# First attention of a two-block transformer: value scratch by token tiles, odd heads' halves swapped when staged, first key load earlier, weight fetches and single operations behind steps

## What is computed

```python
h = rmsnorm(x, g_mix[i])
z = h @ w_in[i]
zb, zc, zx, zq, zk, zv = jnp.split(z, ...)            # 6 x 512 columns
y_c = zb * causal_dwconv3(zc * zx, conv_w[i], conv_b[i])
q = rmsnorm(zq.reshape(b, t, 8, 64), q_norm_g[i])
k = rmsnorm(zk.reshape(b, t, 8, 64), k_norm_g[i])
v = zv.reshape(b, t, 8, 64)
y_a = dilated_attention(q, k, v).reshape(b, t, 512)
y = jnp.concatenate([rmsnorm(y_c, g_out_conv[i]), rmsnorm(y_a, g_out_attn[i])], axis=-1)
x = x + y @ w_out[i]
# then a gated FFN with a causal convolution, a gated per-token embedding,
# and a second block (sparse attention and retention, output product, FFN)
```

## Time and profile before

| | before |
|---|---|
| median of 3 runs | 2587.49 us (2584.89 to 2587.68) |
| profiled execution, its own time | 2583.64 us |
| its span | 2582.0 us |
| busy: PE, DVE, ACT, POOL | 2516.0, 1361.7, 1055.3, 1265.2 us |
| moved by DMA, mean rate | 246.28 MB, 95 GB/s |
| share of PE in the chain that ended last | 87% |

### The profile page before, as it was taken

The page is one execution under the profiler, slowest core; times in us unless marked ns, Lnnn a source line. Parts: engine busy times, 40 slices in busy tenths (PEclk is TensorE's granted clock), DMA queues, the critical chain, the costliest instruction groups (busy, mean ns, idle before and its releaser), DMA issues.

```text
span 2582.0 us, 34606 instructions
## 1 busy us (share of the span) xinstructions
PE 2516.0 (97%) x12210; PEld 2088.5 (81%) x12210; DVE 1361.7 (53%) x2479; ACT 1055.3 (41%) x1951; POOL 1265.2 (49%) x940
## 2 busy tenths in 40 slices
PE   8989999999999999999999999889999999999999
PEld 6877878888888888888877777689888888888887
DVE  5327766188766762225267888777247333333222
ACT  6336653253333332224256666586234333322120
POOL 2122323457766665534525554454356666656441
PEclk9999999999999999999999999999999999999999
DMA  4253432312222244210323212320412222226311
GB/s 157 75 170 117 116 82 83 146 58 106 90 82 88 77 160 175 82 65 27 107 74 94 66 62 70 108 69 21 155 74 74 82 85 79 82 105 222 114 45 70
DMA packets 107402, 246.28 MB, mean 95 GB/s; under 512 B 18880, under 2 KB 40672, under 8 KB 106976
## 3 DMA queue, kind: packets, MB, share of 16 engines
q1 hardware_dynamic: 107232, 244.08, 27.9%
HBM read 184.27 MB, written 55.05 MB: 93 GB/s over the span
## 4 chain that ended last, share of the span: by engine, by line
PE 87%; DVE 4%; ACT 2%; issue 2%; DMA 2%; POOL 2%; SPq 1%; ACTq 0%; DVEq 0%; POOLq 0%
PE PS L965 10%; PE PS L964 10%; PE PS L963 10%; PE PS L701 8%; PE PS L703 8%; PE PS L702 8%; PE PS L981 6%; PE PS L982 6%; PE PS L983 6%; PE PS L1233 2%; PE PS L1213 1%; PE PS L806 1%; PE PS L933 1%; PE PS L935 1%; PE PS L934 1%
## 5 line engine op out<-in xcount | busy, mean ns | idle before, releaser
L701 PE MATMUL PS<-Hh,Wl 128*128 128x512 f32 x1072 | 434.3, 405 | 12.0 <-DVE Hl L1364 9.4
L703 PE MATMUL PS<-Hh,Wh 128*128 128x512 f32 x1072 | 420.7, 392 | 0.0
L702 PE MATMUL PS<-Hl,Wh 128*128 128x512 f32 x1072 | 420.3, 392 | 0.0
L3220 POOL TENSOR_TENSOR Wl<-Wr,Wh 128x512 fp32r<-128x512 f32 (+1 forms) x158 | 209.4, 1346 | 336.0 <-ACT Wh L2320 335.7
L3323 POOL TENSOR_TENSOR RG<-RW,RG 128x512 fp32r<-128x512 f32 x176 | 246.9, 1408 | 130.2 <-ACT RG L2631 130.0
L1807 DVE TENSOR_TENSOR XA<-PS,XA 128x512 f32<-128x512 f32 x192 | 132.4, 691 | 332.5 <-PE PS L983 332.5
L981 PE MATMUL PS<-Hh,RG 128*128 128x512 f32 x704 | 274.1, 389 | 1.6 <-POOL Hl L3419 1.2
L983 PE MATMUL PS<-Hh,RG 128*128 128x512 f32 x704 | 273.9, 389 | 0.0
L982 PE MATMUL PS<-Hl,RG 128*128 128x512 f32 x704 | 273.9, 389 | 0.0
L3323 POOL TENSOR_TENSOR RG<-SW,RG 128x512 fp32r<-128x512 f32 x120 | 165.3, 1377 | 171.5 <-ACT RG L2631 147.0
L965 PE MATMUL PS<-Hh,RG 128*128 128x512 f32 x640 | 249.0, 389 | 0.0
(11 more groups left out here) (365 smaller groups left out, 5145.6 us busy)
## 6 DMA issues: line engine op xcount, KB each, us to landing
RW<-in_wg SPq DMA_DIRECT2D x44, 512.0 KB, 3.7
RW<-in_wu SPq DMA_DIRECT2D x44, 512.0 KB, 4.6
R<-in_wd SPq DMA_DIRECT2D x88, 256.0 KB, 3.0
hgscr<-GB SPq DMA_DIRECT2D x44, 512.0 KB, 2.6
G<-hgscr SPq DMA_DIRECT2D x40, 512.0 KB, 6.8
Wr<-in_wi SPq DMA_DIRECT2D x27, 512.0 KB, 3.4
Wr<-in_wo SPq DMA_DIRECT2D x16, 512.0 KB, 3.3
spill<-X SPq DMA_DIRECT2D x16, 512.0 KB, 2.6
```

What stands on the lines that cost most here:

```text
L701: pe.matmul(ps(b), k.Wl[:, s, wc], xh[:, kx, sl], start=kk == 0, stop=False)
L702: pe.matmul(ps(b), k.Wh[:, s, wc], xl[:, kx, sl], start=False, stop=False)
L703: i = pe.matmul(ps(b), k.Wh[:, s, wc], xh[:, kx, sl], start=False, stop=kk == nk - 1)
L3220: i = pool.tensor_tensor(k.Wl[:, s, c], k.Wr[:, s, c], k.Wh[:, s, c].bitcast(F32), ALU.subtract)
```

## The change

It touches only the first attention and the conv around it. Values: the scratch is laid out by token tile, [tile][token][8 heads x 128], so a store is one row of 896 elements per partition, and every head's load is one DMA of 8 pieces of 128 elements per partition; the swapped order of odd heads is made when VS is written (DVE's one instruction becomes two). SP: `key_load(1)` stands ahead of the values' stores instead of at the first step of `tables1`; the fetch of a unit goes from ahead of c into the tile of half 1 (after its first tick); the store of YC goes into the next j. ACT: `use()` goes from ahead of c into the tile of half 0 (after its first tick); the exponential goes ahead of `next_head`; `key_high` is two halves, at i = 3 and i = 4; the squares go later. DVE: the first tap goes into the tile ("b", 0) and the taps one place on, the second of them into ("b", 1); `conv_b` goes into the tile that follows its own. j = 3 keeps its order. POOL's additions follow the squares.

```diff
@@ vector
     for i in range(8):
         dve.wait_ge(*at("v", i))
         dve.wait_ge(*at("vt_hi", i))
-        dve.scalar_tensor_tensor(out=k.VS[i][:, :, 1, :], in0=ps(i).rearrange("p (h n) -> p h n", h=8),
-                                 scalar=k.sml[:, 112 + i:113 + i], in1=k.VS[i][:, :, 0, :].bitcast(F32), op0=ALU.mult,
-                                 op1=ALU.subtract).then_inc(*up(("free", i), "vt", i))
+        for e in range(2):
+            m = dve.scalar_tensor_tensor(out=k.VS[i][:, e::2, 1 - e, :],
+                                         in0=ps(i).rearrange("p (h n) -> p h n", h=8)[:, e::2, :],
+                                         scalar=k.sml[:, 112 + i:113 + i], in1=k.VS[i][:, e::2, e, :].bitcast(F32),
+                                         op0=ALU.mult, op1=ALU.subtract)
+        m.then_inc(*up(("free", i), "vt", i))
...
         dve.tensor_tensor(zs, ps(b), zs, ALU.mult).then_inc(*up(("free", b), "zx", j, half))
-        if half == 0:
-            return
+
+    def conv_first(j):
         y = k.YC[:, j % 2, :]
...
-                taps = {2: lambda j=j: conv_tap(j, 1), 6: lambda j=j: conv_tap(j, 0)} if (c, half) == ("b", 0) else {}
-                walk(8, 2, taps, tick)
+                later = {}
+                if (c, half) == ("c", 0) and j:
+                    later = {2: lambda j=j, b=b: conv_b(j - 1, 1, b)}
+                if (c, half) == ("b", 0):
+                    if j < 3:
+                        later = {2: lambda j=j: conv_first(j), 6: lambda j=j: conv_tap(j, 1)}
+                    else:
+                        later = {2: lambda j=j: conv_tap(j, 1), 6: lambda j=j: conv_tap(j, 0)}
+                if (c, half) == ("b", 1) and j < 3:
+                    later = {2: lambda j=j: conv_tap(j, 0), 4: lambda j=j, b=b: conv_b(j, 0, b)}
+                walk(8, 2, later, tick)
...
@@ scalar
-        act.activation(k.KSa[h % 2][:, :], k.KSr[:, :], ACT.Copy).then_inc(*up("q_hi", "k1_hi", h))
+        key_part(h, 0)
+        key_part(h, 1).then_inc(*up("q_hi", "k1_hi", h))
+
+    def key_part(h, z):
+        if z == 0:
+            act.wait_ge(*at("k1_in", h, 1))
+        return act.activation(k.KSa[h % 2][:, half_of(z)], k.KSr[:, half_of(z)], ACT.Copy)
...
+        if i == 3 and h < 7:
+            key_part(h + 1, 0)
         if i == 4 and h < 7:
-            key_high(h + 1)
+            key_part(h + 1, 1).then_inc(*up("q_hi", "k1_hi", h + 1))
...
-            if s < n:
-                next_head(s)
             if 1 <= s <= n:
                 e = s - 1
...
+            if s < n:
+                next_head(s)
...
         for c in "cxb":
-            use()
             for half in range(2):
-                walk(8, 2, {}, tick)
+                later = {}
+                if half == 0:
+                    later[2] = use
+                if (c, half) == ("c", 0) and j:
+                    later[6] = lambda j=j: conv_square(j - 1, 1)
+                walk(8, 2, later, tick)
                 b = bank.next()
+                if (c, half) == ("b", 1) and j < 3:
+                    conv_square(j, 0)
...
@@ sync
-        to, src = k.V2[h % 2][:, :, :].bitcast(F32), k.vs[h].rearrange("p (c n) -> p c n", c=8)
-        if h % 2 == 0:
-            sp.dma_start(to, src).then_inc(*up(("d_s", h), "v2_in", h))
-            return
-        for z in range(2):
-            sp.dma_start(to[:, :, 64 - 64 * z:128 - 64 * z], src[:, :, 64 * z:64 * z + 64]).then_inc(
-                *up(("d_s", h), "v2_in" if z else "v2_hi_in", h))
+        src = k.vs.rearrange("c p n -> p c n")[:, :, 128 * h:128 * h + 128]
+        sp.dma_start(k.V2[h % 2][:, :, :].bitcast(F32), src).then_inc(*up(("d_s", h), "v2_in", h))
...
-            if i == 0 and h < 7:
+            if i == 0 and 0 < h < 7:
                 key_load(h + 1)
...
+    key_load(1)
     for i in range(8):
...
-        sp.dma_start(k.vs.rearrange("h p n -> p h n")[:, 1:8, 128 * i:128 * i + 128],
-                     v[:, 128:1024].rearrange("p (h n) -> p h n", h=7)).then_inc(*up(("d_y", i), "v_kept", i))
+        sp.dma_start(k.vs[i][:, 128:1024], v[:, 128:1024]).then_inc(*up(("d_y", i), "v_kept", i))
...
         for c in "cxb":
-            use()
             for half in range(2):
-                walk(8, 2, {}, bg.tick)
+                walk(8, 2, {2: use} if half else {}, bg.tick)
```

More of the change, by code:

```diff
@@ L1568, in vector @@
                     conv_x(j, half, b)
+                    if (j, half) == (3, 1):
+                        conv_first(3)
                 if c == "b":
-                    conv_b(j, half, b)
                     if j == 3:
+                        conv_b(j, half, b)
                         add("conv", 3, half, k.sq_no["conv", half, 3])
@@ L2472, in key_high @@
     def key_high(h):
-        act.wait_ge(*at("k1_in", h, 1))
-        act.activation(k.KSa[h % 2][:, :], k.KSr[:, :], ACT.Copy).then_inc(*up("q_hi", "k1_hi", h))
+        key_part(h, 0)
[4 more added lines that the diff above has]
+        return act.activation(k.KSa[h % 2][:, half_of(z)], k.KSr[:, half_of(z)], ACT.Copy)
     def query_high(h, half):
@@ L2497, in scalar @@
         act.wait_ge(*at("rstd", "mix", i // 4))
-        act.activation(k.VS[i][:, :, 0, :], ps(i).rearrange("p (h n) -> p h n", h=8), ACT.Copy,
+        act.activation(k.VS[i][:, :, :, :].rearrange("p (c e) z n -> p c (e z) n", e=2)[:, :, 0:4:3, :],
+                       ps(i).rearrange("p (c e n) -> p c e n", c=4, e=2), ACT.Copy,
                        scale=k.sml[:, 112 + i:113 + i]).then_inc(*up("hn_a", "vt_hi", i))
@@ L2587, in scalar, with conv_square @@
     bg.add(attention1_norm())
+    def conv_square(j, half):
+        staged = [("v2_in", 0, 7), ("v_kept", 7)] if (j, half) == (1, 0) else []
+        square("conv", j, half, k.YC[:, j % 2, half_of(half)], staged + [("yb", j, half)])
     def y_high(half):
@@ L2599, in scalar @@
         for c in "cxb":
-            use()
             for half in range(2):
-                walk(8, 2, {}, tick)
+                later = {}
[4 more added lines that the diff above has]
+                walk(8, 2, later, tick)
                 b = bank.next()
+                if (c, half) == ("b", 1) and j < 3:
+                    conv_square(j, 0)
                 if c == "b":
-                    staged = [("v2_in", 0, 7), ("v_kept", 7)] if (j, half) == (1, 0) else []
-                    square("conv", j, half, k.YC[:, j % 2, half_of(half)], staged + [("yb", j, half)])
                     if j == 3:
+                        conv_square(3, half)
                         y_high(half)
@@ L3304, in gpsimd @@
                 walk(8, 2, {}, bg.tick)
-                if c == "b" and 0 < j < 3:
-                    add("conv", j, half)
-                    pool.wait_ge(*at("acc", "conv", half, j))
+                if (c, half) == ("b", 1) and 0 < j < 3:
+                    add("conv", j, 0)
+                    pool.wait_ge(*at("acc", "conv", 0, j))
+                if (c, half) == ("c", 0) and 0 < j - 1 < 3:
+                    add("conv", j - 1, 1)
+                    pool.wait_ge(*at("acc", "conv", 1, j - 1))
                 if (c, j) == ("b", 3):
@@ L3689, in sync @@
         for c in "cxb":
-            use()
             for half in range(2):
-                walk(8, 2, {}, bg.tick)
+                walk(8, 2, {2: use} if half else {}, bg.tick)
+                if (c, half) == ("c", 0) and j:
+                    sp.wait_ge(*at("yb", j - 1, 1))
+                    sp.dma_start(d["yscr"][j - 1], k.YC[:, (j - 1) % 2, :]).then_inc(
+                        *up(("d_ys", j - 1), "yc_stored", j - 1))
             if (c, j) == ("x", 3):
@@ L3698, in sync @@
                     sp.dma_start(k.YR[:, kx, :], d["yscr"][kx]).then_inc(*up(("d_y", kx), "y_in", kx))
-        if j < 3:
-            sp.wait_ge(*at("yb", j, 1))
-            sp.dma_start(d["yscr"][j], k.YC[:, j % 2, :]).then_inc(*up(("d_ys", j), "yc_stored", j))
     def gate_up_load(tag, f):
```

## The result

The changed kernel takes 2566.73 us in the median of four runs (2566.01 to 2568.96); the kernel before, measured beside it, 2586.27 us (2584.89 to 2587.68). The ratio is 0.9926 with a 95% interval of 0.9909 to 0.9943: **19.5 us faster**. The forecast was 2568.0 us, and 19.5 us saved. The profiled execution took 2567.04 us.

A forecast was written before the change was run, and what follows sets the result against it. In the first attention the order of other engines' queues, not their throughput, was taken to hold PE back. The terms 9.7 + 3.0 + 7.8 - 1.0 = 19.5 us gave 2587.5 - 19.5 = 2568.0 us, range 2563 to 2577.

The forecast's parts named there:

- the list of PE's waits: From 130 to 420 us PE stands still ten times, 18.0 us in all, mostly for ACT's exponential and DVE's low part.
- The marks that I set: Longest PE wait under 2 us, no DMA wait for head 1's key, clock 1.00 from 165, PE over 98 of 100.
- the claim that PE bounds the rest: After the first attention PE is the bound, so time it gains there should reach the kernel's end.
- Key of head 1: Loading this key ahead of the values' stores removes PE's 7.57 us wait and 2.1 us of slow clock: 9.7 us.
- the second rival: First head: values' traffic makes stores or head 1's query late, some 4 us return, 2572 us; chance 0.11.
- The exponential: Later heads' keys: with key and square no longer ahead of ACT's exponential, PE's waits for it go, 3.0 us.
- Heads' ends: At heads' ends PE's four waits for DVE's low part, 6.3 us, and 1.5 us of slow clock go: 7.8 us.
- What comes in: Second tap and conv_b enter steps 4 to 6 of heads 2 and 5, where DVE has less room: 1.0 us lost.
- a rival for the *first* tap: DVE's first taps run long beside POOL's subtraction at heads' ends; 2.6 us come back, 2570.6 us; chance 0.11.
- What I costed at nothing: DVE's two halves, values' loads and stores, later weights' high part, and SP no longer stopping for POOL: no cost counted.
- The slower rival: Keys of heads 2 to 7 wanted too early at i = 3, 7.42 us each, 2612 us; chance 0.03.
- The values' traffic: First head: full DMA engines make stores or head 1's query late, some 4 us return, 2572 us; chance 0.11.

The follow-up runs named there:

- fetch_alone: The kernel before with only SP's part: the weight's fetch in the walk's second half, the convolution tile's store one step later; 2582.45 us, ratio 0.9984 to before.
- old_fetch: The changed kernel with SP's weight fetch ahead of a head's step again; 2605.38 us, ratio 1.0067 to the kernel before.
- pool_step5: The changed kernel with POOL's low part of the next key asked for at step 5 instead of 4; 2563.97 us, ratio 0.9912 to the kernel before.
- tap_clear: The changed kernel with DVE's second tap one step sooner in its walk (slot 0 instead of 2); 2563.20 us, ratio 0.9910 to the kernel before.
- old_fetch_use: The changed kernel with both SP's weight fetch and ACT's making of the weight's high part ahead of a head's step again; 2577.60 us, ratio 0.9963 to before.
- old_next_head: The changed kernel with the next head's high parts ahead of the exponential again and the key copied whole at i = 4; 2565.62 us, ratio 0.9910 to before.
- old_ends: The changed kernel with DVE's taps and conv_b, ACT's squares and use, and POOL's sums in their old places; 2573.12 us, ratio 0.9946 to before.
- key_alone: The kernel before with only the load of head 1's key moved ahead of the values' stores; 2580.43 us, ratio 0.9966 to before.

## Why the prediction was right, and which steps of it were not

**The sum.** 19.5 us forecast, 19.5 measured, 19.3 in the stage. That holds because the list of PE's waits was read rightly: nine of the ten went, 17.2 us, with the slow clock behind them, and two new ones of 1.7 us came. The marks that I set came out: longest wait 0.93 us (under 2), no wait for the key, granted clock 1.00, PE at 98.09 of 100. By the medians the stage's gain arrives at the end, as the claim that PE bounds the rest has it. That the sum agrees to the tenth is luck: the interval is some 4 us wide either way, the new waits cost 0.7 us more than I allowed, and a small wait of 0.3 us that I had left as it was went.

**The split was wrong**, in four places.

1. *Key of head 1, 9.7 us.* Worth 6.0 and 6.2 us. The step that failed is "what is late next is nothing I can name": with this load alone it is the query of head 1, 2.18 us of PE's time, which the second rival names. In the changed kernel the first head's wait and slow clock go whole, as forecast, but not by this load alone. The rest is likely the later fetch's, which no longer stands ahead of the query, and the values'; fetch_alone takes 1.9 us off the same wait, and no run divides the rest. The key's size was read wrongly too: its load is two DMAs of 0.26 MB and ACT needs both, so it is 0.52 MB; ACT came for it late enough that nothing hung on this.
2. *The exponential, 3.0 us.* The waits go, but not by this edit alone: 0.4 us when it is undone. The square shares the cause, and I put the whole on the key because it stood next to the exponential in the timeline.
3. *Heads' ends less what comes in, 7.8 - 1.0 = 6.8 us.* Undone 9.3 us: PE's waits are 7.5 us longer (the low part's 6.3 us in place of the tap's 1.7, 2.6 us for the exponential, of which I had counted 1.1 under the key and 1.5 stand behind stores of values, and 0.3 us of a small wait) and the slow clock 1.7 us.
4. *What comes in, 1.0 us.* The mechanism was named wrongly. I expected a DVE that is short of room; PE's new waits are 1.74 us and come from POOL holding the tap. I had looked at this collision as a rival for the *first* tap, which takes 0.80 or 0.81 us now in all three places, and not for the second, which I moved in my sum without asking what POOL does beside it. The Trainium skill, in "SBUF — State Buffer", section "SBUF: two separate sides", names a DVE operation with two inputs from SBUF as one that contends with a POOL operation that reads SBUF; the tap is one, and the trace agrees. For the first tap I had expected that it would now be POOL that waits, and so it is: POOL's subtractions that begin while a first tap runs, at 214.64, 289.64 and 364.38, take 1.65, 1.48 and 1.62 us, where most others of their size take 1.29 or 1.30.

**What I costed at nothing.** SP's fetch. "SP no longer stops in front of a head for POOL, so tables, keys and queries come sooner" had the right direction and no price. Alone it saves 3.8 us in the stage, and without it the change would have lost 17 us by the times. The slower rival had the right picture, ACT's loads late with the probabilities queued behind, and named only a part of the cause: in old_fetch ACT waits 31.3 us for the query and 18.1 for the key, behind SP's wait for POOL, which ACT's later high part lengthens; with the key's step undone most of the loss is still there. My sentence against that rival, that the fetch ahead of the key is gone, is what decided it.

**The other rivals.** That the first tap still gets in the way did not happen. The values' traffic does make ACT wait, 2.06 us, until 172.1 where I had it through by 169; PE does not wait for it in the changed kernel's trace and waits 0.4 and 0.8 us in two with the same first head (pool_step5, tap_clear), less than the 4 us of the rival. Open is how the loss of old_fetch_use divides between the key's earlier step and the faster heads' ends. ACT waits 11.9 us in six for the key there and 6.7 for the query; in the kernel before it was 7.6 us, 7.4 of them for head 1, and 5.0. That points at the key's step, but no run has the old step with `Wh` and fetch both ahead.

## What to carry to other kernels

Where one engine's queue waits for another's result before it issues loads, ask what makes that result later: an edit that costs its own engine nothing can hold up every load behind the wait, and a part with no price in the sum can be the one that the rest stands on. A sum over waits can be right while its split over edits is wrong, because two operations ahead of the same wait share it; undoing each part shows that, and measuring the stage in the trace can resolve what a median of runs cannot, if the traced execution's own time lies near that median. To move work out of another engine's way, move the one that is not waiting for something: moving POOL's place in its program changed nothing, since its start is set by ACT.

## What the runs showed of the hardware that I had not expected

**How exactly the tap is held.** In head 5 of the changed kernel POOL ends at 302.16 and the tap at 303.23:

```profile
299.75 2.41 POOL L3300 TENSOR_TENSOR KSa<-KSr,KSa 64x1024 fp32r<-64x1024 f32 x1 [4.74 <-ACT KSa L2494]
...
300.53 2.70 DVE L1542 SCALAR_TENSOR_TENSOR YC<-ZC,cols,YC 128x1024 f32<-128x1024 f32 x1
```

In the two collisions here and the two in old_next_head the tap ends 1.07 to 1.09 us after POOL, however much of it lay beside (it takes 1.63, 2.00, 2.36 or 2.70 us). So it does not share: but for some 0.2 us of its 1.28 it gets nothing done until POOL is done, and the profile shows that time as busy and not as a wait. It is the same the other way round: POOL's three lengthened subtractions end 1.15 or 1.16 us after the first tap beside them. DVE's reduction at 225.64 above, whose input is in PS, ran at 0.55 us beside the same POOL operation.

**The clock after equal waits.** Before, the wait of 1.96 us at 252.42 was followed by granted clocks of 0.73 and 0.50. In the same execution a wait of 2.01 us, and in old_ends one of 1.94 us like that at 252.42, were not:

```profile
331.57 1.07 PE L806 MATMUL PS<-mats,PP 128*128 128x128 f32 x8 [2.01 <-DVE PT L1433]
...
320.00:340.00 20.00, 17.89 (x105) 14.47 (x104) 11.50 (x24) 11.93 (x27) 6.36 (x5) 1.00 0.39 122
```

and old_ends:

```profile
242.72 1.07 PE L806 MATMUL PS<-mats,PP 128*128 128x128 f32 x8 [1.94 <-DVE PT L1436]
...
240.00:260.00 20.00, 18.05 (x105) 14.92 (x104) 12.66 (x27) 13.28 (x33) 6.19 (x4) 1.00 0.43 142
```

The granted clock is 1.00 over the 20 us around each. What a wait costs in clock is not fixed by its length: 5.1 us of slow clock stood in the stage before, none in key_alone with 14.0 us of waits, among them two of 1.96 and 1.99 us at the heads' ends. What else decides it is not shown here.
